# Attention weights transposed by VectorE in 32x32 blocks, and value products in groups of 32 partitions

## The reference

```python
def masked_softmax(s, mask, sink=None):
    ...
    return p / jnp.where(den > 0, den, 1.0)

    # NSA, one block of 128 queries: compressed, selected and window branch
    p_c = masked_softmax(s_c, dist_c >= 0)
    o_c = jnp.einsum('bgrqc,bgcd->bgrqd', p_c.astype(v_cmp.dtype), v_cmp)
    ...
    p_s = masked_softmax(s_s, (dist_s >= 0)[:, :, None])
    o_s = jnp.einsum('bgrqm,bgqmd->bgrqd', p_s.astype(v_g.dtype), v_g)
    ...
    o_w = jnp.einsum('bgrqs,bsgd->bgrqd', p_w.astype(v_w.dtype), v_w)
    out = gb[:, 0] * o_c + gb[:, 1] * o_s + gb[:, 2] * o_w
    # SWA
    pr = masked_softmax(s, mask[None, :, None, None], sink)
    o = jnp.einsum('bngrqk,bnkgd->bnqgrd', pr.astype(vb.dtype), vb)
```

## Time and profile before

| | |
|---|---|
| time, median of 3 runs | 1002.2 us (1001.81 to 1002.37) |
| span of the profiled execution, first to last instruction | 999.8 us |
| TensorE busy | 983.0 us, 98% |
| VectorE busy | 692.9 us, 69% |
| GpSimd busy | 452.3 us, 45% |
| ScalarE busy | 425.5 us, 43% |
| attention stage, from the first full iteration to the last value product | 384.62 to 526.96 us of the span |

### The profile page before, as it was taken

The page is one execution under the profiler, slowest core; times in us unless marked ns, Lnnn a source line. Parts: engine busy times, 40 slices in busy tenths (PEclk is TensorE's granted clock), DMA queues, the critical chain, the costliest instruction groups (busy, mean ns, idle before and its releaser), DMA issues.

```text
span 999.8 us, 19627 instructions
## 1 busy us (share of the span) xinstructions
PE 983.0 (98%) x7920; PEld 799.7 (80%) x7920; DVE 692.9 (69%) x1160; ACT 425.5 (43%) x829; POOL 452.3 (45%) x511
## 2 busy tenths in 40 slices
PE   6999999999999999999999999999999999999997
PEld 5787777777777777777778888888889998888886
DVE  3799796565566956546556882269887865489987
ACT  4134432322314334546555444545444443345563
POOL 3366557254334766656683448446222234510000
PEclk9999999999999999999999999999999999999999
DMA  9345533122223564112113636433322333244452
GB/s 262 89 129 151 122 92 68 24 65 65 67 66 98 157 159 137 49 50 56 52 54 122 193 116 229 131 127 106 106 85 86 112 106 109 86 136 170 157 176 99
DMA packets 149459, 111.48 MB, mean 112 GB/s; under 512 B 21190, under 2 KB 132048, under 8 KB 149369
## 3 DMA queue, kind: packets, MB, share of 16 engines
q1 hardware_dynamic: 145644, 104.16, 35.7%
q10 hardware_dynamic: 3692, 6.07, 2.2%
q0 software_dynamic: 32, 0.00, 0.0%
HBM read 99.70 MB, written 10.52 MB: 110 GB/s over the span
## 4 chain that ended last, share of the span: by engine, by line
PE 86%; DVE 10%; issue 1%; DMA 1%; POOL 1%; ACT 1%; SPq 0%; DVEq 0%; ACTq 0%
PE ps L2318 33%; PE ps L2798 5%; PE ps L2797 5%; PE ps L2802 5%; PE ps L2332 4%; PE ps L2438 3%; PE ps L2683 3%; PE ps L2858 2%; PE ps L2860 2%; PE ps L2859 2%; PE ps L2625 2%; PE ps L2835 2%; PE ps L2832 2%; PE ps L2831 2%; DVE XF L1430 2%
## 5 line engine op out<-in xcount | busy, mean ns | idle before, releaser
L2318 PE MATMUL ps<-HLO,WHI 128*128 128x512 f32 x440 | 178.2, 405 | 0.4 <-issue 0.4
L2318 PE MATMUL ps<-HHI,WHI 128*128 128x512 f32 x440 | 175.5, 399 | 1.0 <-DVE HLO L1462 0.7
L773 POOL TENSOR_TENSOR WLO<-WRAW,WHI 128x1024 fp32r<-128x1024 f32 (+1 forms) x52 | 104.2, 2006 | 106.5 <-ACT WHI L888 106.5
L869 POOL TENSOR_TENSOR WLO<-WRAW,WHI 128x512 fp32r<-128x512 f32 x50 | 72.3, 1453 | 118.8 <-ACT WHI L1230 117.5
L2318 PE MATMUL ps<-HHI,WLO 128*128 128x512 f32 x440 | 118.1, 398 | 0.0
L777 POOL CAST WHI<-WRAW 128x256 fp32r<-128x256 f32 (+1 forms) x133 | 62.7, 472 | 106.5 <-PE ps L2318 106.3
L808 POOL TENSOR_TENSOR WLO<-WRAW,WHI 128x256 fp32r<-128x256 f32 x132 | 105.6, 800 | 10.7
L2318 PEld LDWEIGHTS ps<-HHI,WHI 128*128 128x128 f32 x440 | 82.6, 188 | 23.2 <-issue 4.7
L2318 PEld LDWEIGHTS ps<-HLO,WHI 128*128 128x128 f32 x440 | 82.6, 188 | 22.7 <-issue 5.1
L2318 PEld LDWEIGHTS ps<-HHI,WLO 128*128 128x128 f32 x440 | 80.5, 188 | 18.3 <-issue 1.4
L2798 PE MATMUL ps<-HLO,WHI 128*128 128x512 f32 x200 | 77.9, 389 | 0.0
(11 more groups left out here) (517 smaller groups left out, 2404.1 us busy)
## 6 DMA issues: line engine op xcount, KB each, us to landing
WRAW<-in_w_in SPq DMA_DIRECT2D x47, 512.0 KB, 4.4
WRAW<-in_w_gate SPq DMA_DIRECT2D x22, 512.0 KB, 3.8
WRAW<-in_w_up SPq DMA_DIRECT2D x22, 512.0 KB, 3.9
WRAW<-in_w_down SPq DMA_DIRECT2D x19, 512.0 KB, 3.4
spilled<-SQ SPq DMA_DIRECT2D x24, 256.0 KB, 2.4
GATES<-spilled SPq DMA_DIRECT2D x6, 768.0 KB, 4.8
WRAW<-in_w_in SPq DMA_DIRECT2D x16, 256.0 KB, 3.7
WRAW<-in_w_branch SPq DMA_DIRECT2D x32, 128.0 KB, 2.9
```

What stands on the lines that cost most here:

```text
L773: return pool.tensor_tensor(lo[:, 0:chunks, :], WRAW[:, n % NRAW, 0:chunks, :], hi[:, 0:chunks, :].bitcast(F32), ALU.subtract)
L869: pool.tensor_tensor(lo, raw_half(item[1], item[2]), hi.bitcast(F32), ALU.subtract).then_inc(w_lo, 1)
L2318: last = pe.matmul(DB[g % 2][:, :], (wlo if which == "low" else whi)[:, c, :], lo if which == "x_low" else hi, start=a == 0, stop=a == 3 * ...
```

## The change

The weights are no longer turned by TensorE. VectorE turns them with its own transpose, which works within blocks of 32x32: `turned(n-2)` takes the place of `first_half(n-2)` and rewrites the whole EB slot of the step in place (both groups, up to 1024 elements a partition). ScalarE's `second_half` is gone. A block of 32 keys by 32 queries then lies with its keys on the same 32 partitions on which its queries had been, and the 32 partitions number a hold query group a for all keys. A value product therefore has 32 rows: values of 32 keys by 64 channels on partitions 32a to 32a+31, times weights of two heads by 32 queries (64 columns). It runs for each of the 4 query groups a, both g and each group r of 32 keys, and writes to bank R[2+a]. The values are needed on all four partition groups, so they are copied by 16 small DMAs each into V4 (NSA, token block 0 from ScalarE's queue, the rest from SyncE's) and SV4 (SWA, from SyncE's queue). The compressed values go through VC4 and ECBT in the same way.

The 36 steps become 28 value-product "events": where a step has one head, two steps (heads j and j+1) share an event, and the order of the steps puts them behind each other. EB has six slots. `pv` stands between `qk(n)` and the dense chunks. The four output banks are the same for all query blocks, so the first event of a block waits for `group_out` of the block before it; `group_out` is now four instructions, and ScalarE runs it ahead of `exps(n)`.

```diff
-    STEPS += [("nsa", _i, tuple(range(_j, _j + _nj)), _b) for _j in range(0, 4, _nj) for _b in range(2)]
+    for _pair in range(0, 4, 2):
+        STEPS += [("nsa", _i, tuple(range(_j, _j + _nj)), _b) for _b in range(2) for _j in range(_pair, _pair + 2, _nj)]
...
+EVENTS = []
+for _n in range(NST):
+    _kind, _i, _j, _b = STEPS[_n]
+    if len(_j) == 1 and _j[0] % 2:
+        EVENTS[-1] += (_n,)
+    else:
+        EVENTS.append((_n,))
+EVENT_OF = {_n: _e for _e, _steps in enumerate(EVENTS) for _n in _steps}
+EVENT_AT = {_steps[-1]: _e for _e, _steps in enumerate(EVENTS)}
+SCORED = [n for n in range(NST) if STEPS[n][0] != "cmp"]
+NEB = 6
+SLOT = {n: m % NEB for m, n in enumerate(SCORED)}
+HELD = {n: SCORED[m - NEB] for m, n in enumerate(SCORED) if m >= NEB}
...
                     sp.wait_ge(gn_ok, 4)
                     spilled_before(sp, SW0 + 6)
                     sp.dma_start(SWQ[:, :, :], spilled[0:6].rearrange("b p t -> p b t")).then_inc(swq_in, 16)
+                if n == ATT_JOB + 1:
+                    sp.wait_ge(vtok_ok, 2)
+                    for a in range(4):
+                        for b in range(4):
+                            sp.dma_start(V4[rows32(a), b, :, 1:4, :], VST[rows32(b), :, 1:4, :]).then_inc(v4_rest, 16)
+                if n == SINK_JOB:
+                    sp.wait_ge(vtok_ok, 4)
+                    sp.wait_ge(sc_ok, 2 * HALF_DONE + 2)
+                    for a in range(4):
+                        for b in range(4):
+                            sp.dma_start(SV4[rows32(a), :, b, :, :], SVST[rows32(b), :, :].rearrange("p (h k) n -> p h k n", h=2))\
+                                .then_inc(sv4_in, 16)
...
             for n in range(NST + 3):
                 if n < NST and STEPS[n][0] == "swa":
-                    pool.wait_ge(p_T, n - 2)
+                    pool.wait_ge(pv_mm, EVENT_OF[HELD[n]] + 1)
                     js, w = STEPS[n][2], keys_of(n) + 1
-                    pool.tensor_copy(EB[:, n % 3, :, 0:w * len(js)].rearrange("p g (j c) -> p g j c", c=w)[:, :, :, w - 1:w],
...
             def group_out(o):
-                act.wait_ge(pv_mm, GROUP_END[o] + 1)
-                act.activation(O[:, 1 + o // 4, :, P * (o % 4):P * (o % 4) + P],
-                               R[4 + o % 2][:, :].rearrange("p (a b) -> p a b", a=4), ACT.Copy).then_inc(o_ev, 1)
+                act.wait_ge(pv_mm, EVENT_OF[GROUP_END[o]] + 1)
+                for a in range(4):
+                    t0 = P * (o % 4) + 32 * a
+                    last = act.activation(O[:, 1 + o // 4, :, t0:t0 + 32],
+                                          R[2 + a][:, 0:P].rearrange("p (j t) -> p j t", j=4), ACT.Copy)
+                last.then_inc(o_ev, 1)
 
             for n in range(NST + 4):
+                if n - 4 in GROUP_END:
+                    group_out(GROUP_END.index(n - 4))
                 if n < NST:
                     exps(n)
-                if 2 <= n < NST + 2:
-                    second_half(n - 2)
-                if n - 4 in GROUP_END:
-                    group_out(GROUP_END.index(n - 4))
                 if LAST_CMP < n <= LAST_CMP + 4:
                     sink_high(n - LAST_CMP - 1)
 
...
                 kind, i, j, b = STEPS[n]
                 dve.wait_ge(qk_mm, n + 1)
-                if n >= 3:
-                    dve.wait_ge(p_T, n - 2)
+                if n in HELD:
+                    dve.wait_ge(pv_mm, EVENT_OF[HELD[n]] + 1)
+                if kind != "cmp" and SLOT[n] == NEB - 1 and n not in HELD:
+                    dve.wait_ge(v4_first, 256)
+                    dve.wait_ge(v4_rest, 256)
...
-            def first_half(n):
-                dve.wait_ge(p_T, n + 1)
-                if n >= 2:
-                    dve.wait_ge(pv_mm, n - 1)
-                w = keys_of(n) * max(1, len(STEPS[n][2]))
-                dve.tensor_copy(PTB[:, n % 2, 0, 0:w], R[2][:, 0:w]).then_inc(pt_dve, 1)
+            def turned(n):
+
+                dve.wait_ge(p_ok, n + 1)
+                if STEPS[n][0] == "cmp":
+                    if n:
+                        dve.wait_ge(pv_mm, EVENT_OF[n])
+                    dve.transpose(ECBT[:, :, :, :].rearrange("p g j c -> p (g j c)"),
+                                  ECB[:, :, :, :].rearrange("p g j c -> p (g j c)")).then_inc(pt_ok, 1)
+                    return
+                w = keys_of(n) + (STEPS[n][0] == "swa")
+                p = EB[:, SLOT[n], :, 0:w * len(STEPS[n][2])].rearrange("p g (j c) -> p g j c", c=w)[:, :, :, 0:keys_of(n)]
+                dve.transpose(p, p).then_inc(pt_ok, 1)
 
             for n in range(NST + 3):
                 if n == NSA_STEPS:
@@ -1839,7 +1883,7 @@
                 if 1 <= n < NST + 1:
                     weights(n - 1)
                 if 2 <= n < NST + 2:
-                    first_half(n - 2)
+                    turned(n - 2)
                 if LAST_CMP + 1 < n <= LAST_CMP + 5:
...
-            def p_transpose(n):
-
-                pe.wait_ge(p_ok, n + 1)
-                if n:
-                    pe.wait_ge(pt_dve, n)
-                    pe.wait_ge(pt_act, n)
-                for g in range(2):
-                    if STEPS[n][0] == "cmp":
-                        last = tr(R[2 + g][:, 0:P], ECB[:, g, :, :].rearrange("p j c -> p (j c)"))
-                        continue
-                    for jj in range(len(STEPS[n][2])):
-                        at0, to = (head_cols(n, jj, s).start for s in (STEPS[n][0] == "swa", 0))
-                        for k in range(keys_of(n) // P):
-                            last = tr(R[2 + g][:, to + k * P:to + k * P + P], EB[:, n % 3, g, at0 + k * P:at0 + k * P + P])
-                last.then_inc(p_T, 1)
-
-            def pv(n):
-
+            def pv(e):
+
+                n = EVENTS[e][0]
                 kind, i, j, b = STEPS[n]
                 o = group_of_step(n)
-                pe.wait_ge(pt_dve, n + 1)
-                pe.wait_ge(pt_act, n + 1)
-                opens = n == 0 or group_of_step(n - 1) != o
-                if opens and o >= 2:
-                    pe.wait_ge(o_ev, o - 1)
-                bank = R[4 + o % 2]
+                opens = e == 0 or group_of_step(EVENTS[e - 1][0]) != o
+                pe.wait_ge(pt_ok, EVENTS[e][-1] + 1)
+                if opens and o:
+                    pe.wait_ge(o_ev, o)
                 if kind == "cmp":
-                    for m in range(4):
+                    for a in range(4):
                         for g in range(2):
-                            last = pe.matmul(bank[half[g], m * P:(m + 1) * P], VCZ[:, m, g, :], PTB[:, n % 2, g, 0:P],
-                                             start=m == 0, stop=False, skip_group_check=True)
-                else:
-                    kb = keys_of(n) // P
-                    if kind == "swa" and n == NSA_STEPS:
-                        pe.wait_ge(vtok_ok, 4)
-                    for jj in range(len(j)):
-                        to = head_cols(n, jj).start
-                        for k in range(kb):
+                            last = pe.matmul(R[2 + a][half[g], 0:P], VC4[rows32(a), g, :], ECBT[rows32(a), g, :, :],
+                                             start=True, stop=False, skip_group_check=True)
+                    last.then_inc(pv_mm, 1)
+                    return
+                if kind == "nsa" and i < 2:
+                    pe.wait_ge(*((v4_rest if i else v4_first), 256))
+                if n == NSA_STEPS:
+                    pe.wait_ge(sv4_in, 256)
+                w = keys_of(n) + (kind == "swa")
+                cols = slice(32 * j[0], 32 * j[0] + 64)
+                kb = keys_of(n) // P
+                for k in range(kb):
+                    t = i + 1 - kb + k
+                    for r in range(4):
+                        at0 = P * k + 32 * r
+                        for a in range(4):
                             for g in range(2):
-                                last = pe.matmul(bank[half[g], j[jj] * P:(j[jj] + 1) * P], VT[:, b, i + 1 - kb + k, half[g]],
-                                                 PTB[:, n % 2, g, to + k * P:to + (k + 1) * P],
-                                                 start=opens and jj == 0 and k == 0, stop=k == kb - 1, skip_group_check=True)
+                                values = V4[rows32(a), r, b, t, half[g]] if kind == "nsa" else SV4[rows32(a), t // 2, r, t % 2, half[g]]
+                                if len(j) == 2:
+                                    p = EB[rows32(a), SLOT[n], g, 0:2 * w].rearrange("p (j c) -> p j c", c=w)[:, :, at0:at0 + 32]
+                                else:
+                                    p = EB[rows32(a), SLOT[n]:SLOT[n] + 2, g, at0:at0 + 32]
+                                last = pe.matmul(R[2 + a][half[g], cols], values, p, start=opens and k == 0 and r == 0,
+                                                 stop=k == kb - 1 and r == 3, skip_group_check=True)
                 last.then_inc(pv_mm, 1)
 
             for n in range(NST + 3):
```

(28 more changed lines are left out.)

55 lines of the change are left out of this document (28 added, 27 removed).

## The result

The changed kernel takes 1033.27 us (median of 4 runs, 1032.12 to 1034.63), the kernel before 1002.0 us on the same chip. The ratio is 1.0314, 95% interval 1.0301 to 1.0328: slower, where the prediction had 983.4 us. The profiled execution has a span of 1031.4 us, 31.6 more than before.

A forecast was written before the change was run, and what follows sets the result against it. TensorE was taken to bound the kernel (busy 983.0 of 999.8 us). Work of -26.5 us plus waits of 3.5, 3.2 and 1.0 gave -18.8 us, so 983.4 us; 8-in-10 range 977 to 999.

The forecast's parts named there:

- The 32 DMAs of values and 16 of sink values need no price in the sum: Value loading: DMAs issued ten or more us ahead of use cost nothing; even 5 us apiece would not turn the sign.
- A record costs 58/8 = 7.3 ns: New value products on TensorE: each place engaged some 58 ns, eight places at once; 25.2 us in all.
- partly fed: Rival, value-product bursts: queue may not supply instructions fast enough; 11.2 ns a record, +13.5 us, 997 us; chance 0.14.
- -26.5 of work: TensorE in the attention stage: new work of 30.2 us against 56.7 removed, so 26.5 us less to do.
- transposes: VectorE's transposes, priced at the pace of its PSUM copy: 1.2 us for 1024 elements, 0.96 for 768.
- borders: New query blocks: TensorE's first event waits for ScalarE's `group_out`; 0.65 us twice and 1.1 twice, sum 3.5 us.
- Waits for VectorE's transposes: TensorE behind iterations without an event: 0.5 us four times at i = 3, 0.2 four times at i = 2; 3.2 taken.
- GpSimd's 1.0: Two-head steps: GpSimd near TensorE's 3.6 us, in SWA 0.2 more; about 0.1 over ten steps, 1.0 us.
- Four at once: Rival, value products: at most four places run together; 15.2 ns a record, +27.3 us, 1011 or 1009 us; chance 0.10.
- VectorE as the bound: Rival, two-head steps and i = 3: VectorE's transpose takes 2.3 us; +12 us, 995 us; chance 0.08.
- The floor: Rival, value products: small records held apart whatever their place, up to 28.4 ns; +73 us, 1056 us; chance 0.03.

The follow-up runs named there:

- before_dma: Kernel before the change, with 16 small DMAs added on ScalarE's queue ahead of the high parts of the keys: 1010.66 us, ratio 1.0091 to the kernel before.
- dma_late: Changed kernel, with ScalarE's 16 value DMAs issued behind its high parts of keys and queries: 1021.73 us, ratio 1.0204 to the kernel before.
- half_keys: Changed kernel without half of its value products (output not the layer's): 989.51 us.
- fill128: Kernel before the change, with 128 tiny products of constants added on TensorE ahead of each step's transposes: 1232.54 us.
- spread: dma_late, with the value products of steps with 384 and 512 keys mostly divided over two iterations: 1012.97 us, ratio 1.011 to the kernel before.
- both: spread (which contains dma_late), plus pairs of two-head steps sharing an event so products stream 128 columns: 996.7 us, ratio 0.9946 to the kernel before.
- half_n8: half_keys, with each value product streaming 8 columns instead of 64 (output not the layer's): 991.88 us.
- both_merged: both, with its 32 DMAs of NSA values merged into 16 carrying all four token blocks, half on each queue: 997.21 us, ratio 0.9955 to the kernel before.

## Why the prediction was wrong

The span was to shrink by 18.8 us and grew by 31.6: 50.4 us to explain.

- **"The 32 DMAs of values and 16 of sink values need no price in the sum": wrong.** I looked at the landing, which is 3.0 us in the median here and hidden, and not at the issue. I looked at what is ahead of their use and not at what is queued behind them on ScalarE. `before_dma` measures 9.0 us, `dma_late` 11.5. Of a DMA's issue the Trainium skill, page "DMA: Bandwidth & Descriptors", section "Anatomy of one DMA — SWDGE (gpsimd) path", gives some 50 ns of sequencer dispatch, for GpSimd's path; ScalarE's queue here takes about 620 ns for each of these.
- **"A record costs 58/8 = 7.3 ns": right for the first 32 records of a burst, wrong for the rest.** Measured 11.3 on average, 10.7 in the cleanest bursts, which over 3456 records is 12 to 14 us more. The scaling that was clean from two to four places does go on to eight: records 17 to 32 come every 7.3 ns. But I took a pace from bursts of 32 records and used it for 64 to 256, and behind the 32nd record it is 11 to 13 ns in most bursts. That is my rival "partly fed" in its doubt and in its number (11.2); it was put at 997, since it had nothing for stops, issues and clock. What sets the slower pace isn't shown.
- **No price for the supply of instructions: the step that failed most.** I named it as a doubt in that rival ("no row shows whether the queue supplies instructions twice as fast for so long") but priced it as a slower pace. It comes as whole stops at the borders of packets, nine of them 1.5 to 2.4 us long, 22.0 us in all. `half_keys`, `fill128` and `spread` show it from three sides: half of the instructions, one short stop; idle instructions alone, stops; the same instructions more evenly, a third less.
- **The clock: not in the prediction.** In the stage, -26.5 of work, 13.8 for the pace, 22.0 of stops and 3.2 of waits give 12.5 against 23.2 measured. The half clock explains most of the 10.7 left over. In the stage 229 dense matmuls are busy for 71.1 us, where 235 took 65.5 before: 7.3 us more for the same number. The scores take 3.5 us more. Of these 10.8 us, 2.65 lie in three pieces at the start of the stage (those of `before_dma`, the same lengths). Smaller terms nearly cancel: six dense matmuls have left the stage (-1.6), and there are 1.2 of waits before scores and 0.7 for cmp.
- **Right in mechanism: transposes and borders.** Transposes measured 1.22 and 0.96 us, against 1.2 and 0.96. Waits for VectorE's transposes were to be 3.2 us and are 1.6, for `group_out` 3.5 and 1.6, and GpSimd's 1.0 doesn't appear. All are less, since longer iterations gave the others time; in `both`, whose iterations are shorter, TensorE's waits for the transposes grow to 4.0.
- **The rivals.** Four at once needed 15.2 ns and VectorE as the bound 2.3 us a transpose: neither. The floor by the Trainium skill's figure, page "TensorE: Matmul & The Clock Gate", of about 25 ns between starts doesn't hold across places: it gave 86 us for records that took 39. But its idea, that a small product has a cost that its size doesn't give, does. So says the Trainium skill's page "TensorEngine Tiling (Array Packing)" too, section "Instruction Overhead", that one column takes as long as 60: in `half_n8` an eighth of the columns leaves records 17 to 32 at 7.3 ns and saves 11% of a burst.

What stays open: what slows the records behind the 32nd, and why some borders of packets stop a burst and others don't. That TensorE waits for the packet itself is inferred from the place of the stops, from the times of the packets and from the three runs, and not seen directly.

## What to carry to other kernels

Count instructions, not only matmul time: where 32x64 products replace 128x128 ones, TensorE's work shrank by more than half on paper, while four instructions a product outran their supply: all four bursts of 256 records, two of four of 192 and three of ten of 128 stopped for some 2 us. Don't carry a pace over to bursts longer than the one that it was measured on. Spread such bursts between long matmuls, and let one product do more columns. Before a series of small DMAs goes on a compute engine's queue, look at what stands behind it in that engine's program, and price 0.6 us an issue, or what the trace shows for DMAs of that shape.

## What I hadn't expected of the hardware

- TensorE's instructions arrive in packets of 16 KB, 256 instructions, never closer than 3.3 us in any run. A burst at 10.7 ns a record, two instructions each, uses 256 in 1.4 us; what is in store carries it over 134 to 235 records at i = 3, to the border of a packet, and then TensorE stops for about 2 us.
- Inside a burst on eight places the first 32 records are quicker than the rest: 7.3 ns a record for the 17th to 32nd, 11.5 behind.
- Six of nine stops that short are followed by 3.4 or 6.8 us at 1.2 instead of 2.4 GHz, in which six dense matmuls take 2.5 to 2.9 us instead of 1.59.
- A DMA of 32 partitions by 1 KB costs its issuing engine 0.62 us of its own time, and one of 4 KB rows no more (`both_merged`: 0.59 to 0.61 each for the first four). It isn't the size: SyncE issues `spilled<-SQ` of 256 KB in 0.34 us in the same trace.
- VectorE's 32x32 transpose of float32 costs 1.05 ns an element above 0.15 us, as a copy does.
